# Moving the relative bias products, the first sparse attention jobs and two scalings in a one-core three-block kernel

## The chip, the cores and the metric

The kernel runs on one core of one Trainium2 chip. The metric is the device time of one launch in microseconds (us); lower is better. The core's engines are TensorE (PE in the rows; its weight loads are PEld), VectorE (DVE), ScalarE (ACT), GpSimd (POOL) and SyncE (SP), which here only issues DMAs. Each has its own queue of instructions and waits for the others through semaphores.

## The reference, cut to what matters

The input is 512 tokens of 1024 channels in float32. Three residual mixers follow each other, each with a gated feed-forward behind it:

```python
x = x + conformer_conv(rmsnorm(x))       # pointwise, GLU, 31-tap conv, layer norm, swish, pointwise
x = x + swiglu(rmsnorm(x))
x = x + dilated_attention(rmsnorm(x), rel_bias)   # 12 heads, relative bias from a table of 32 buckets
x = x + swiglu(rmsnorm(x)); x = rmsnorm(x)        # the final norm of the first block
# second block
rq, rk, rv, rg, aq, ak, av, iq, ik, iw = split(rms_norm(h) @ w_in)
ret_out = retention(rq, rk, rv, rg)      # per head: rms over 64 channels, then times silu(rg)
att_out = dsa_attention(aq, ak, av, iq, ik, iw)   # an indexer keeps the top 128 keys per query
h = h + rms_norm(concat(ret_out, att_out) @ w_out)
h = h + rms_norm(swiglu(conv3(rms_norm(h) @ w_up)) @ w_down)
```

## The kernel before, in words

Activations lie transposed: 128 channels on the partitions, 512 tokens on the free axis, eight tiles of X. Every float32 product of the big layers is made of three reduced-precision ones (hi by hi, lo by hi, hi by lo; lines 620 to 622), so that every weight is split: ScalarE copies it to `W_hi` (line 1154), VectorE subtracts to get `W_lo` (line 1821). A layer is a list of units of 256 columns; a unit has two halves of 128 columns, and each half runs over its 8 tiles of the contraction. The weights of a unit are loaded, split and used two units apart.

**Slots.** The last mixer's input layer "inp" has 13 units. PE's order there is written by hand: after each tile k of half h of unit j, a function `beside(g)` is called with the slot number g = 16j + 8h + k, and it issues what else belongs to that slot. ScalarE and VectorE call functions of the same name with the same g, in the same order, and put the evictions of a half (`raw_copy`, `taken`) behind its eighth slot. Nothing ties the engines to a common time but semaphores: each engine works through its own list in order.

**Sparse attention jobs.** There are 16 jobs n (four blocks of 128 queries times four pairs of heads, keys 128, 256, 384 and 512 wide). Job n begins at slot s(n) = 84 + 7n. Its scores are at s+1 on PE, the masked maximum at s+2 on VectorE, the exponentials at s+3 on ScalarE, the reciprocal at s+4 on VectorE and the scaling at s+4 on ScalarE. Its transposes lie at the next job's s and s+2, with ScalarE copies at s+1 and s+3, and its values at the next job's s+4 (PE) with a copy out (ScalarE).

**Beside them** stand, with slots of their own: 48 rounds of the top-k search on VectorE (`choose`, lines 2264 and 2266, slots 66 to 157; 256 keys wide for the first 16 rounds, then 384, then 512), and the retention: scores on PE (line 1045), decay on VectorE (`ret_decay`, line 2301), values on PE (line 1056); after the fourth of each head pair ScalarE takes the sum out (`ret_take`, line 1557, slots 147, 162, 189, 200), PE sums over the heads (`head_sum`, line 1064, slots 148, 163, 190, 201), ScalarE makes the root, and VectorE the reciprocal (`ret_normed`, line 2307, slots 150, 165, 192, 203). The vector queue makes `W_lo` for the unit after next in the slots with g % 16 == 2, ahead of all else in the slot; ScalarE makes `W_hi` at the end of each unit, behind the eviction copy.

```python
                if g % SLOTS == 2 and g > 2 * SLOTS:      # vector, beside(g)
                    split_lo(L, At(g // SLOTS - 1))
                ...
                if r == 2 and 0 <= q < 16:
                    dsa_max(q)
                ...
                if r == 3 and 0 <= q < 16:                # scalar, beside(g)
                    dsa_exp(q)
                ...
                if g - 1 in RET_LAST_AT:
                    ret_take(RET_LAST_AT.index(g - 1))
```

**The bias products** (line 708, three products of a 33 x 4 table with a 33 x 384 one-hot matrix, six matmul records) are issued on PE behind the last tap of the 31-tap convolution and ahead of the layer norm's sums (lines 761, 763, 770). ScalarE copies them out (line 1298), sends them to DRAM (line 1313), loads the Sqrt table and squares the centred tiles. PE waits for the three copies before the first sum of squares. The result is first read for the second mixer.

**The end of "wout"**, the last mixer's output layer: VectorE copies each half to Y (line 2389), multiplies X by the final norm's gain and factor two tiles per unit (line 2412), the last two of them between the two halves of the last `W_lo` (line 2421) and the norm's reciprocal (line 2432), and then adds the normed result to X (lines 2443 and 2446).

Of the kernel before, what the change touches and what calls it, by code (L numbers as in the profile page):

```python
# [7 lines left out]
ACT = mybir.ActivationFunctionType  # L8
# [48 lines left out]
DIAG = 384  # L57
# [56 lines left out]
STAT_AT = SLOTS + 5  # L114
KV_AT = 2 * SLOTS + 4
INDEX_AT = [52, 54, 58, 60, 62, 64, 66, 68, 70, 72, 74, 76]
DSA_AT, DSA_STRIDE = 84, 7
ROUND_AT = [66 + 39 * r // 20 for r in range(48)]
RV_AT = [129, 130, 177, 178]
RET_AT = [134, 137, 140, 143, 149, 152, 155, 158, 180, 182, 184, 186, 191, 193, 195, 197]  # L120
# [56 lines left out]
def build(nc, a, out):  # L177
# [13 lines left out]
    with ctx:  # L191
# [417 lines left out]
        def _(pe):  # L609
# [91 lines left out]
            def bias_products():  # L701

                pe.wait_ge(tab_in, 32)
                pe.wait_ge(pads_set, 2)
                pe.wait_ge(const2_in, 16)
                pe.wait_ge(acc_free, layers["pw2"].base)
                for g in range(3):
                    nc.tensor.matmul(PS[1 + g][0:GROUP_HEADS, 0:DIAG], table[:, GROUP_HEADS * g:GROUP_HEADS * (g + 1)],
                                     onehot[:, g, :], start=True, stop=True).then_inc(fvec_ps, 1)

            def conv_tap(n):
# [44 lines left out]
                            conv_tap(g - FIRST_TAP)  # L756
            for n in range(SLOTS * L.n - FIRST_TAP, len(PE_TAPS)):
                conv_tap(n)
            bias_products()
            pe.wait_ge(ln_sum, 7)  # L760
            nc.tensor.matmul(PS[0][:], ones, SSUM[:], start=True, stop=False)
            pe.wait_ge(conv_made, 6)
            nc.tensor.matmul(PS[0][:], ones, CV[:, 7, :], start=False, stop=True).then_inc(ln_sum_ready, 1)
            pe.wait_ge(fvec_made, 3)
            for n, m in enumerate(LN_SUMS):
                if m == LN_PAIR:
                    pe.wait_ge(xc_made, DT + 1)
                else:
                    pe.wait_ge(xc_sq, m + 1)
                nc.tensor.matmul(PS[1][:], ones, LN_SQ[m % 4], start=(n == 0), stop=(n == len(LN_SUMS) - 1)).then_inc(ln_var_ready, 1)  # L770
            linear("pw2", HID_hi, HID_lo, ready=after(ln_lo_made, 0))

            def three_units(L):
# [292 lines left out]
            def beside(g):  # L1066

                if g == STAT_AT:
                    pe.wait_ge(ssum2, 8)
                    nc.tensor.matmul(AUX[1][:], ones, SSUM2[:], start=True, stop=True).then_inc(stat2_ready, 1)  # L1070
                    rms_sum(FINAL)
                if g == KV_AT:
                    kv_transposes()
                if g in INDEX_AT:
                    index_scores(INDEX_AT.index(g))
                if g in RV_AT:
                    rv_transposes(RV_AT.index(g))
                if g in HEADSUM_AT:
                    head_sum(HEADSUM_AT.index(g))
                if g in RET_LAST_AT:  # L1080
                    ret_values(4 * RET_LAST_AT.index(g) + 3)
                if g in RET_AT:
                    n = RET_AT.index(g)
                    if n % 4:
                        ret_values(n - 1)
                    ret_scores(n)
                q, r = divmod(g - DSA_AT, DSA_STRIDE)
                if r == 0 and 1 <= q <= 16:
                    dsa_transposes(q - 1, 0)
                if r == 1 and 0 <= q < 16:  # L1090
                    dsa_scores(q)
                if r == 2 and 1 <= q <= 16:
                    dsa_transposes(q - 1, 1)
                if r == 4 and 1 <= q <= 16:
                    dsa_values(q - 1)
# [62 lines left out]
        def _(act):  # L1158
# [136 lines left out]
            def take_bias(g):  # L1295

                act.wait_ge(fvec_ps, g + 1)
                nc.scalar.activation(fvec[:, g, :], PS[1 + g][0:GROUP_HEADS, 0:DIAG], ACT.Copy).then_inc(fvec_made, 1)

            for g in range(SLOTS, SLOTS * L.n):  # L1300
                beside_pw1(g)
# [5 lines left out]
                if g >= SLOTS * L.n:  # L1307
                    diagonals(c)
            split_hi(act, L, At(L.n - 1))
            for g in range(3):  # L1310
                take_bias(g)
            act.wait_ge(fvec_made, 3)
            act.dma_start(bias_rows.rearrange("(g h) d -> h g d", h=GROUP_HEADS), fvec[:]).then_inc(rows_out, 16)

            warm_table(ACT.Sqrt)
            for m in range(DT):
                act.wait_ge(xc_made, m + 1)
# [3 lines left out]
            act.wait_ge(ln_var_ready, len(LN_SUMS))  # L1321
            nc.scalar.activation(STD[:], PS[1][:], ACT.Sqrt, bias=epst[:], scale=1.0 / D_MODEL).then_inc(ln_std, 1)
            warm_table(ACT.Silu)
            for m in range(DT):
                act.wait_ge(ln_scaled, m + 1)
                nc.scalar.activation(CV[:, m, :], CV[:, m, :], ACT.Silu, bias=vec("ln_b", m), scale=vec("ln_g", m)).then_inc(ln_act, 1)
                act.wait_ge(ln_act, m + 1)
                nc.scalar.activation(HID_hi[:, m, :], CV[:, m, :], ACT.Copy).then_inc(ln_hi_made, 1)
# [244 lines left out]
            def beside(g):  # L1573

                if g == STAT_AT:
                    act.wait_ge(stat2_ready, 1)
                    nc.scalar.activation(STD[:], AUX[1][:], ACT.Sqrt, bias=eps2t[:], scale=1.0 / D_MODEL).then_inc(std2_made, 1)
                    act.wait_ge(stat_ready, FINAL + 1)
                    nc.scalar.activation(RF[:], AUX[0][:], ACT.Sqrt, bias=epst[:], scale=1.0 / D_MODEL).then_inc(std_made, 1)
                if g - 1 in INDEX_AT:  # L1580
                    index_relu(INDEX_AT.index(g - 1))
                if g - 1 in RV_AT:
                    rv_copy(RV_AT.index(g - 1))
                q, r = divmod(g - DSA_AT, DSA_STRIDE)
                if r == 1 and 1 <= q <= 16:
                    dsa_keys_first(q - 1, 0)
                if r == 3 and 1 <= q <= 16:
                    dsa_keys_first(q - 1, 1)
                if r == 3 and 0 <= q < 16:
                    dsa_exp(q)  # L1590
                if r == 4 and 1 <= q <= 16:
                    dsa_out(q - 1)
                if r == 4 and 0 <= q < 16:
                    dsa_scaled(q)
                if g - 1 in RET_LAST_AT:
                    ret_take(RET_LAST_AT.index(g - 1))
                if g - 1 in HEADSUM_AT:
                    ret_std(HEADSUM_AT.index(g - 1))
                if g == GATE_AT:
                    gate(11, 0)  # L1600
                    gate(11, 1)
                    gate(12, 0)
# [189 lines left out]
        def _(dve):  # L1792
# [525 lines left out]
            def beside(g):  # L2318

                if g % SLOTS == 2 and g > 2 * SLOTS:  # L2320
                    split_lo(L, At(g // SLOTS - 1))
                if g == KV_AT + 1:
                    kv_tokens()
                if g == 3 * SLOTS + 12:
                    nc.vector.tensor_scalar(LEFT0[:], later, -NEG, None, ALU.mult).then_inc(mask_made, 1)
                q, r = divmod(g - DSA_AT, DSA_STRIDE)
                if r == 2 and 0 <= q < 16:
                    dsa_max(q)
                if r == 4 and 0 <= q < 16:
                    dsa_reciprocal(q)  # L2330
                if g in RET_AT:
                    ret_decay(RET_AT.index(g))
                if g - 2 in HEADSUM_AT:
                    ret_normed(HEADSUM_AT.index(g - 2))
                if g in ROUND_AT:
                    choose(ROUND_AT.index(g))
# [38 lines left out]
            def y_steps(name, y0, add):  # L2375
# [2 lines left out]

                def step(j):
                    u = j.plus(L.base)  # L2380
                    for half in range(2):
                        dve.wait_ge(acc_ready, u.v(2, half + 1))
                        m = At(2 * j.c + half, None if j.i is None else j.i * 2)
                        y = Y[:, bass.ds(m.v(), 1), :].rearrange("p o n -> p (o n)")
                        ps = PS[2 * u.parity + half][:]
                        if add:
                            i = nc.vector.tensor_tensor(y, ps, y, ALU.add)
                        else:
                            i = nc.vector.tensor_copy(y, ps)
                        i.then_inc(x_half, 1) if y0 is None else i.then_inc(y_ready, 1)  # L2390
                    if y0 is None:
                        dve.wait_ge(x_half, j.v(2, 16 + 2))
                    else:
                        dve.wait_ge(y_ready, j.v(2, y0 + 2))
                    nc.vector.sem_inc(acc_free, 1)
                    if name != "wout" or j.c < L.n - 1:
                        split_lo(L, j)
                    if name == "wout" and j.c < L.n - 1:
                        final_normed(j.c)
# [26 lines left out]
            def add_normed(n, gain, k, tiles, split):  # L2426

                if split:
                    final_scaled(DT - 2)
                    last_lo(0)  # L2430
                dve.wait_ge(std_made, n + 1)
                nc.vector.reciprocal(R4[:], STD4[:]).then_inc(r_made, 1)
                if split:
                    final_scaled(DT - 1)
                    last_lo(1)
                dve.wait_ge(r_ps, TOKEN_NORMS.index(n) + 1)
                if k == 0:
# [173 lines left out]
```

## Time and profile before

| | |
|---|---|
| median of 3 runs | 1819.21 us (1819.13 to 1819.86) |
| the profiled execution | 1819.52 us |
| its span, first to last instruction | 1817.7 us |
| mean granted TensorE clock | 0.989 |
| PE busy | 1765.9 us of the span |
| DVE, ACT, POOL busy | 1029.6, 707.8, 172.1 us |
| DMA | 164.63 MB, mean 91 GB/s |

The profile is of one execution. A timeline row gives start, duration, engine, line, operation, tiles and, in brackets, how long the engine had stood idle before and what released it. The granted clock is a share of 2.4 GHz. Some 52 us of the span lie outside PE's busy time, the launch and the end among them.

### The profile page before, as it was taken

Reading aid. Unit: us, or ns where it says so; the run is one execution under the profiler, and the core shown is the slowest. Engines: PE = TensorE matmul, PEld = TensorE weight load, DVE = VectorE, ACT = ScalarE, POOL = GpSimd, SP = SyncE. Lnnn points to the kernel's source line nnn. Section 1 sums busy time; section 2 is a strip of 40 time slices with the busy share of each in tenths; the row PEclk is TensorE's granted clock in tenths of the full one; section 3 lists DMA queues with packets and bytes.
Section 4 is the critical chain, followed back from the end, with each engine's and each line's share of the span. In section 5 each row is a group of like instructions: output and inputs, shape, how many; then the busy total and the mean of one; then the engine's idle time right before and its main releaser. Section 6 shows DMA issues by size and latency. Waiting matters only on the chain.

```text
span 1817.7 us, 21121 instructions
## 1 busy us (share of the span) xinstructions
PE 1765.9 (97%) x8106; PEld 1404.2 (77%) x8106; DVE 1029.6 (57%) x1287; ACT 707.8 (39%) x1095; POOL 172.1 (9%) x128
## 2 busy tenths in 40 slices
PE   7999799999999999999999999989999899999997
PEld 6887588888888878778888888756557778888886
DVE  6998664433444555654424444559856677537753
ACT  5655532212233344332212323465564444324431
POOL 0010010000000100110000004471200200000001
PEclk9999999999999999999999999999999999999998
DMA  5210322322232311132312231523112122322221
GB/s 181 70 47 28 99 94 101 115 95 83 102 118 78 124 70 53 65 105 103 127 70 93 92 127 70 153 73 116 50 62 70 70 93 101 119 70 92 101 96 47
DMA packets 28052, 164.63 MB, mean 91 GB/s; under 512 B 4511, under 2 KB 5675, under 8 KB 11596
## 3 DMA queue, kind: packets, MB, share of 16 engines
q1 hardware_dynamic: 25088, 158.11, 24.7%
q10 hardware_dynamic: 2892, 5.55, 1.0%
q8 instruction: 47, 0.77, 0.2%
q14 instruction: 25, 0.20, 0.0%
HBM read 156.28 MB, written 4.47 MB: 88 GB/s over the span
## 4 chain that ended last, share of the span: by engine, by line
PE 88%; DVE 8%; ACT 2%; issue 1%; POOL 1%; DMA 0%; DVEq 0%; SPq 0%; ACTq 0%; POOLq 0%
PE PS L620 26%; PE PS L622 26%; PE PS L621 26%; PE PS L726 1%; PE PS L727 1%; PE PS L725 1%; DVE W_lo L1821 1%; DVE WK L2266 1%; DVE SSUM L2307 1%; DVE TOP L2264 1%; PE PS L1045 1%; ACT W_hi L1154 1%; POOL ISC L1765 1%; PE PS L1056 1%; DVE PS L2443 0%
## 5 line engine op out<-in xcount | busy, mean ns | idle before, releaser
L620 PE MATMUL PS<-H_hi,W_hi 128*128 128x512 f32 x1600 | 641.6, 401 | 18.3 <-DVE H_lo L1801 14.0
L622 PE MATMUL PS<-H_hi,W_lo 128*128 128x512 f32 x1600 | 626.1, 391 | 0.0
L621 PE MATMUL PS<-H_lo,W_hi 128*128 128x512 f32 x1600 | 625.6, 391 | 0.0
L1154 ACT ACTIVATE W_hi<-W_raw 128x2048 fp32r<-128x2048 f32 (+2 forms) x130 | 262.6, 2020 | 674.2 <-PE PS L622 674.2
L620 PEld LDWEIGHTS PS<-H_hi,W_hi 128*128 128x128 f32 x1600 | 301.9, 189 | 105.1 <-issue 41.2
L1821 DVE TENSOR_TENSOR W_lo<-W_raw,W_hi 128x2048 fp32r<-128x2048 f32 (+2 forms) x130 | 331.2, 2548 | 59.5 <-ACT W_hi L1154 59.1
L622 PEld LDWEIGHTS PS<-H_hi,W_lo 128*128 128x128 f32 x1600 | 301.5, 188 | 64.6
L621 PEld LDWEIGHTS PS<-H_lo,W_hi 128*128 128x128 f32 x1600 | 302.2, 189 | 59.5 <-issue 1.2
L620 PE MATMUL PS<-HID_hi,W_hi 128*128 128x512 f32 x640 | 250.3, 391 | 7.5 <-DVE HID_lo L1962 7.4
L622 PE MATMUL PS<-HID_hi,W_lo 128*128 128x512 f32 x640 | 249.7, 390 | 0.0
L621 PE MATMUL PS<-HID_lo,W_hi 128*128 128x512 f32 x640 | 249.7, 390 | 0.0
L1695 POOL TENSOR_TENSOR SSUM<-SSUM,SQ 128x512 f32<-128x512 f32 x43 | 65.5, 1522 | 1345.9 <-ACT SQ L1196 1344.1
L620 PEld LDWEIGHTS PS<-HID_hi,W_hi 128*128 128x128 f32 x640 | 120.7, 189 | 34.0 <-issue 8.5
L621 PEld LDWEIGHTS PS<-HID_lo,W_hi 128*128 128x128 f32 x640 | 120.6, 188 | 25.0
L622 PEld LDWEIGHTS PS<-HID_hi,W_lo 128*128 128x128 f32 x640 | 120.6, 188 | 25.1
L2004 DVE TENSOR_TENSOR T_u<-PS,R 128x512 f32<-128x512 f32 x44 | 30.4, 690 | 155.7 <-PE PS L622 155.7
L2012 DVE TENSOR_TENSOR T_hid<-T_u,T_act 128x512 f32<-128x512 f32 x66 | 45.7, 693 | 81.1 <-ACT T_act L1378 78.5
L1977 DVE TENSOR_TENSOR X<-X,PS 128x512 f32<-128x512 f32 x40 | 27.0, 684 | 113.9 <-PE PS L622 113.7
L1386 ACT ACTIVATE HID_hi<-T_hid 128x512 f32 (+1 forms) x66 | 42.0, 636 | 57.7 <-DVE T_hid L2012 57.7
L1267 ACT ACTIVATE D_hi<-cmat,tap_hi 128x128 fp32r<-128x128 f32 x108 | 42.1, 390 | 32.2 <-PE PS L727 31.5
L1801 DVE SCALAR_TENSOR_TENSOR H_lo<-X,vecs,H_hi 128x512 fp32r<-128x512 f32 x40 | 36.2, 914 | 27.4 <-ACT H_hi L1181 27.2
L1870 DVE SCALAR_TENSOR_TENSOR CV<-U,vecs,CV 128x512 f32<-128x512 f32 x66 | 50.1, 759 | 0.1
(289 smaller groups left out, 1522.0 us busy)
## 6 DMA issues: line engine op xcount, KB each, us to landing
W_raw<-in_inp SPq DMA_DIRECT2D x13, 1024.0 KB, 4.8
W_raw<-in_pw SPq DMA_DIRECT2D x11, 1024.0 KB, 4.8
W_raw<-in_gu0a SPq DMA_DIRECT2D x11, 1024.0 KB, 4.8
W_raw<-in_gu0b SPq DMA_DIRECT2D x11, 1024.0 KB, 4.8
W_raw<-in_gu1a SPq DMA_DIRECT2D x11, 1024.0 KB, 4.8
W_raw<-in_gu1b SPq DMA_DIRECT2D x11, 1024.0 KB, 4.8
W_raw<-in_gu2a SPq DMA_DIRECT2D x11, 1024.0 KB, 4.8
W_raw<-in_gu2b SPq DMA_DIRECT2D x11, 1024.0 KB, 4.8
```

The lines of the kernel that those rows point to most:

```text
L620: nc.tensor.matmul(dst[:], wh, x_hi[:, k, :], start=(k == first), stop=False)
L621: nc.tensor.matmul(dst[:], wh, x_lo[:, k, :], start=False, stop=False)
L622: return nc.tensor.matmul(dst[:], wl, x_hi[:, k, :], start=False, stop=(k == last))
L1154: nc.scalar.activation(W_hi[b][:, 0:n], W_raw[b][:, 0:n], ACT.Copy).then_inc(w_hi, 1)
L1267: last = nc.scalar.activation(dst[c % 3][:, x, :], ident, ACT.Copy, scale=w)
L1386: nc.scalar.activation(dst, T_hid[:], ACT.Copy).then_inc(hid_hi_made, 1)
L1695: nc.gpsimd.tensor_tensor(SSUM[:], SSUM[:], SQ[:, m.parity, :], ALU.add).then_inc(ss_made, 1)
L1801: nc.vector.scalar_tensor_tensor(out=dst, in0=src, scalar=scale, in1=hi, op0=ALU.mult, op1=ALU.subtract).then_inc(h_lo_made, 1)
L1821: nc.vector.tensor_tensor(W_lo[b][:, 0:n], W_raw[b][:, 0:n], W_hi[b][:, 0:n].bitcast(F32), ALU.subtract).then_inc(w_lo, 1)
L1870: i = nc.vector.scalar_tensor_tensor(out=dst, in0=src, scalar=w, in1=dst, op0=ALU.mult, op1=ALU.add)
L2004: nc.vector.tensor_tensor(T_u[:], PS[2 * b + 1][:], R[:], ALU.mult).then_inc(acc_free, 1)
L2012: nc.vector.tensor_tensor(T_hid[:], T_u[:], T_act[:], ALU.mult).then_inc(hid_made, 1)
```

## The change

Three things change. The bias products are issued behind the layer norm's sums of squares and go to PSUM banks 2 to 4 (they went to 1 to 3), ScalarE's copies and the DMA stand behind the layer norm's root and the loading of the Silu table, and PE waits for the copies ahead of the layer "pw2". The first four sparse attention jobs begin at slots 94, 99, 104 and 109, the others at 116 + 7(n - 4), four slots later than before. The last two scalings of X are issued ahead of the wait for the last unit of "wout".

```diff
-DSA_AT, DSA_STRIDE = 84, 7
+DSA_STARTS = [94, 99, 104, 109] + [116 + 7 * n for n in range(13)]
+DSA_SLOT = {s + r: (n, r) for n, s in enumerate(DSA_STARTS) for r in range(5)}
...
-                    nc.tensor.matmul(PS[1 + g][0:GROUP_HEADS, 0:DIAG], table[:, GROUP_HEADS * g:GROUP_HEADS * (g + 1)],
+                    nc.tensor.matmul(PS[2 + g][0:GROUP_HEADS, 0:DIAG], table[:, GROUP_HEADS * g:GROUP_HEADS * (g + 1)],
...
-            bias_products()
             pe.wait_ge(ln_sum, 7)
...
-            pe.wait_ge(fvec_made, 3)
             for n, m in enumerate(LN_SUMS):
...
+            bias_products()
+            pe.wait_ge(fvec_made, 3)
             linear("pw2", HID_hi, HID_lo, ready=after(ln_lo_made, 0))
...
-                q, r = divmod(g - DSA_AT, DSA_STRIDE)
+                q, r = DSA_SLOT.get(g, (-1, -1))
...
             split_hi(act, L, At(L.n - 1))
-            for g in range(3):
-                take_bias(g)
-            act.wait_ge(fvec_made, 3)
-            act.dma_start(bias_rows.rearrange("(g h) d -> h g d", h=GROUP_HEADS), fvec[:]).then_inc(rows_out, 16)
...
             warm_table(ACT.Silu)
+            for g in range(3):
+                take_bias(g)
+            act.wait_ge(fvec_made, 3)
+            act.dma_start(bias_rows.rearrange("(g h) d -> h g d", h=GROUP_HEADS), fvec[:]).then_inc(rows_out, 16)
...
                 def step(j):
                     u = j.plus(L.base)
+                    if name == "wout" and j.c == L.n - 1:
+                        final_normed(j.c)
...
                 if split:
-                    final_scaled(DT - 2)
                     last_lo(0)
...
                 if split:
-                    final_scaled(DT - 1)
                     last_lo(1)
```

The lookup `DSA_SLOT.get` replaces the `divmod` on PE, ScalarE and VectorE alike.

## Rows read from the trace of the kernel before

**Rows 1.** The page, its fourth part: the chain that ended last, by engine

```profile
PE 88%; DVE 8%; ACT 2%; issue 1%; POOL 1%; DMA 0%; DVEq 0%; SPq 0%; ACTq 0%; POOLq 0%
```

**Rows 2.** Waits of PE from 1150 to 1425 us: total, times, longest

```profile
PE PS L1012 <- ACT E L1530: 7.9, 4, 5.2
PE PS L1056 <- DVE A L2301: 2.3, 2, 1.5
...
PE PS L1064 <- ACT RQK L1558: 0.5, 1, 0.5
```

**Rows 3.** Stretches: length, busy and count per engine, granted clock, DMA share, GB/s

```profile
1220.00:1225.00 5.00, 5.00 (x15) 3.44 (x16) 2.50 (x11) 1.20 (x7) 3.05 (x3) 0.50 0.22 54
1301.00:1304.00 3.00, 3.00 (x10) 1.35 (x12) 1.50 (x4) 0.00 (x0) 0.96 (x1) 0.50 0.25 60
1385.00:1392.00 7.00, 7.00 (x33) 5.79 (x32) 5.79 (x8) 3.22 (x4) 0.00 (x0) 1.00 0.00 0
```

**Rows 4.** Timeline around the layer norm's sums, all engines

```profile
169.90 1.30 POOL L1717 TENSOR_TENSOR SSUM<-SSUM,CV 128x512 f32<-128x512 f32 x1 [2.02 <-DVE CV L1889]
...
177.56 2.10 PE L708 MATMUL PS<-onehot,table 33*4 33x384 f32 x6
177.74 0.69 DVE L1889 TENSOR_TENSOR CV<-CV,PS 128x512 f32<-128x512 f32 x1 [1.29 <-PE PS L727]
...
179.05 0.48 ACT L1298 ACTIVATE fvec<-PS 4x384 f32<-4x384 f32 x1 [0.17 <-PE PS L708]
...
180.55 1.02 PE L763 MATMUL PS<-CV,cmat 128*128 128x512 f32 x2
...
181.69 4.87 DVE L1943 SCALAR_TENSOR_TENSOR CV<-PS,CV 128x512 f32<-128x512 f32 x8 [3.26 <-PE PS L763]
...
194.93 0.81 ACT L1326 ACTIVATE CV<-CV,vecs 128x512 f32<-128x512 f32 x1 [2.63 <-DVE CV L1954]
```

**Rows 5.** Timeline at the end of the layer "wout", VectorE and PE

```profile
1425.32 0.69 DVE L2389 COPY Y<-PS 128x512 f32<-128x512 f32 x1 [3.46 <-PE PS L622]
...
1428.49 0.72 DVE L2412 SCALAR_TENSOR_TENSOR X<-X,vecs,RF 128x512 f32<-128x512 f32 x1
1428.62 1.16 PE L685 MATMUL PS<-cmat,R 128*128 128x128 f32 x8 [0.57 <-DVE R L2432]
1429.12 1.22 DVE L2421 TENSOR_TENSOR W_lo<-W_raw,W_hi 128x1024 fp32r<-128x1024 f32 x1
1430.26 0.75 DVE L2443 SCALAR_TENSOR_TENSOR PS<-Y,vecs,PS 128x512 f32<-128x512 f32 x1
```

**Rows 6.** From the eviction of slot 79's half to slot 98: one stretch, then timeline

```profile
1210.80:1232.60 21.80, 16.60 (x70) 11.65 (x69) 16.74 (x46) 9.80 (x22) 13.12 (x10) 0.84 0.29 85
...
1218.60 0.69 DVE L2207 TENSOR_TENSOR RQK<-PS,CS 128x512 f32<-128x512 f32 x1 [0.63 <-ACT T_act L1492]
1219.21 0.15 DVE L2289 RECIPROCAL RDEN<-DEN 128x2 f32<-128x2 f32 x1
1219.85 0.48 PE L1012 MATMUL PS<-cmat,E 128*128 128x128 f32 x1 [5.20 <-ACT E L1530]
...
1230.37 2.28 DVE L1821 TENSOR_TENSOR W_lo<-W_raw,W_hi 128x2048 fp32r<-128x2048 f32 x1
...
1242.58 1.90 ACT L1154 ACTIVATE W_hi<-W_raw 128x2048 fp32r<-128x2048 f32 x1
```

**Rows 7.** Timeline around the first head sum, slots 142 to 149

```profile
1279.36 0.57 ACT L1522 ACTIVATE E<-PS,NEGMAX 128x384 f32<-128x384 f32 x1
...
1280.26 0.49 PE L1045 MATMUL PS<-RQK 64*128 64x128 f32 x4
...
1284.24 0.60 ACT L1557 ACTIVATE SSUM<-PS 128x512 f32<-128x512 f32 x1 [0.19 <-PE PS L1056]
...
1285.07 3.37 DVE L1821 TENSOR_TENSOR W_lo<-W_raw,W_hi 128x2048 fp32r<-128x2048 f32 x1
...
1285.96 0.59 PE L1064 MATMUL PS<-SSUM,cmat 128*128 128x512 f32 x1
...
1289.74 0.56 DVE L2283 CUSTOM_DVE_ANT_0 PS<-PS,LEFT 128x384 f32<-128x384 f32 x1
```

More of the change, by code:

```diff
@@ L1297, in take_bias @@
                 act.wait_ge(fvec_ps, g + 1)
-                nc.scalar.activation(fvec[:, g, :], PS[1 + g][0:GROUP_HEADS, 0:DIAG], ACT.Copy).then_inc(fvec_made, 1)
+                nc.scalar.activation(fvec[:, g, :], PS[2 + g][0:GROUP_HEADS, 0:DIAG], ACT.Copy).then_inc(fvec_made, 1)
             for g in range(SLOTS, SLOTS * L.n):
@@ L1583, in beside @@
                     rv_copy(RV_AT.index(g - 1))
-                q, r = divmod(g - DSA_AT, DSA_STRIDE)
+                q, r = DSA_SLOT.get(g, (-1, -1))
                 if r == 1 and 1 <= q <= 16:
@@ L2325, in beside @@
                     nc.vector.tensor_scalar(LEFT0[:], later, -NEG, None, ALU.mult).then_inc(mask_made, 1)
-                q, r = divmod(g - DSA_AT, DSA_STRIDE)
+                q, r = DSA_SLOT.get(g, (-1, -1))
                 if r == 2 and 0 <= q < 16:
```

## The prediction

> **What bounds the kernel now.** I read the chain that ended last first: it lies on PE for 88% and on VectorE for 8% [rows 1], so a part of the change counts only where PE stops or where VectorE stands in the chain. Then PE's waits in the last mixer: 7.9 us in four waits for the scaled exponentials, 5.2 of them at once, 2.3 for retention's decay and 0.5 at a head sum [rows 2]. Then stretches for what a wait costs behind it: after the wait of 5.2 the granted clock is 0.50, half of 2.4 GHz, over the 5 us from 1220, and 0.50 again after the waits near 1300 [rows 3]; 5 us at half cost 2.5 us of work. Where PE only multiplies at the full clock, 33 matmuls touch 7.00 us [rows 3], so a slot of three takes about 0.69 us. Last the timelines of the places that the edits touch, to see which queue is late there.
>
> **Bias products.** Now six matmuls run from 177.56 for 2.1 us, while VectorE's last tile of the convolution is complete at 177.74 + 0.69 = 178.43; the matmul that needs it starts only at 180.55, and 1.14 us later VectorE centres the tiles [rows 4]. The other operand of the sums is older: GpSimd's last addition ended at 171.2 [rows 4]. Without the bias products that matmul starts near 178.6, so 1.9 us go (at most 2.1, the products themselves; at least 1.6, if a weight load follows the wait). Everything up to the first Silu moves along. Put back, the products lie in PE's idle time behind the sums of squares, and cost PE nothing. ScalarE's three copies (0.48 each with 0.17 before it, 2.0 together) and a DMA issue of about 0.3 fall into the 2.63 us in which it waits before the first Silu at 194.93 [rows 4]. If that cover were gone, the overhang would be paid in full; 0.3 us at most. Term: **-1.9**.
>
> **Scalings of X.** In the wait of 3.46 us before the copy at 1425.32 there is room for both. Now the second scaling starts at 1428.49, the half of W_lo behind it at 1429.12, and the first multiplication of the norm at 1430.26 [rows 5]. Taken out, it frees 0.63 us, but the multiplication also reads the spread factor, which PE finishes at 1428.62 + 1.16 = 1429.78 [rows 5]: late next. So 0.4 us go (0.3 to 0.6). The first scaling was hidden by ScalarE's copy and stays worth nothing. Term: **-0.4**.
>
> **Sparse attention jobs.** No work is added. What changes is which part of another queue PE must wait for, so I take the places in order.
>
> *The transposes of job 0.* They were at slot 91 and needed VectorE up to slot 88; now they are at slot 99 and need the reciprocal at slot 98, behind that slot's W_lo. From the eviction at 1210.8 to the end of that W_lo at 1232.6 VectorE was busy for 16.74 of 21.8 us [rows 6]. I take 4.3 of the 5.1 us as waits for pieces of jobs 0 and 1 and the rest as gaps between short instructions, and 0.7 of the work is no longer in front. So it gets there at 1227.6 at the earliest, and PE 0.64 later (from reciprocal to transposes, 1219.21 to 1219.85 [rows 6]): 1228.3. PE stood at the transposes from 1219.85 - 5.20 = 1214.65. Without the early scores (0.5) but with 0.3 more wait for an eviction it is through slot 91 at 1214.4, and with four slots and the scores at 1217.6. There it needs the eviction of slot 87, which began at 1218.60 behind 0.6 of waiting and the 0.4 of a maximum [rows 6], and will end at 1218.4: 0.8 of wait. Four slots on, at 1221.2, it stands at the transposes: a wait of **7.1** where 5.2 was, with the same half clock behind it. At the stride of 5 only one slot is left between scaling and transposes, which costs job 2 another 0.3; and its second copy now stands behind the raw copy (0.6) and W_hi (1.90 [rows 6]) of the unit that ends at slot 111 and takes 0.3 itself, where PE needs 1.5 for two slots and a transpose: 1.3. Together 7.1 + 0.8 + 0.3 + 1.3 = 9.5 (6 to 11).
>
> *The first head sum, slot 148.* This is the heart of the forecast. ScalarE takes retention's sum out at slot 147. Before, no job stood directly in front. Now job 8 begins at 144: its exponentials are at 147, ahead of the take, and wait for its maximum at slot 146, which stands behind that slot's W_lo. From the start of retention's scores at 1280.26 to W_lo at 1285.07 are 4.8 us, 4.7 without a reciprocal. Then follow W_lo 3.4, the maximum 1.1 (two of 0.56), the exponentials 1.1 (two of 0.57) and the take 1.1 (two of 0.60, overlapped) with 0.2 for hand-overs [rows 7]: 11.6 in all. PE got to its head sum 5.7 us after the scores (1285.96 - 1280.26 [rows 7]); with the other pieces that now lie between, 6.0. A wait of 5.6. W_lo took 3.37 here and 2.28 at 1230.37 [rows 6, 7]; with 2.28 the wait is 4.5. I take **5.0**, between the two.
>
> The Trainium skill, "SBUF — State Buffer", section "SBUF: two separate sides", says that a VectorE operation with two SBUF inputs and a GpSimd one lock each other out of a shared pair of ports for a whole instruction. By that rule the long W_lo is one that met GpSimd's rotation of the same unit, and the sum is 0.6 higher if they meet again and 0.5 lower if not.
>
> Behind this wait comes a half clock as after the 5.2: 2.5. VectorE stands still meanwhile, since the next decay needs scores that PE issues after the head sum; that may add a us at the values of slot 155, which I leave to the range.
>
> *Both places together.* New: waits 9.5 + 5.0, half clock 2.5 + 2.5, 19.5 in all. Old: the waits for exponentials 7.9 and the longest for a decay 1.5 [rows 2], half clock 2.5 behind the first and some 1.3 for the 3 us at 1301 [rows 3], 13.2 in all. Term: **+6.3** (1 to 11).
>
> *The later head sums.* At slot 162 the take stands behind job 9's scaling, and this behind a reciprocal that follows W_lo. If the queues are level there as in rows 7, W_lo 2.3, reciprocal 0.2, scaling 1.2, take 1.1 and hand-overs 0.2 make 5.0 against PE's 3.7 for three slots and two products: **+1.3** (0 to 2.5). At slot 189 it stands behind job 13's second copy and job 14's exponentials, which are wider than those of rows 7: some 3.3 us against PE's 1.7, +1.6. In return the second decay wait (0.8 of the 2.3) and the wait at the last head sum (0.5) go [rows 2], because no values and copy-out stand before the last take: **+0.3** (-1.3 to 2; three Silus now stand behind the last job's copy-out ahead of the next layer's input, and can cost up to 1).
>
> **Sum.** -1.9 - 0.4 + 6.3 + 1.3 + 0.3 = +5.6, so 1819.5 + 5.6 = **1825.1 us**, against the profiled execution's 1819.52. That one lies 0.3 above the median, 1819.21, which is nothing beside these terms.
>
> **Rivals.** (a) *Faster.* The wait of 5.2 and its half clock go and nothing takes their place: VectorE works through the rounds without stopping for jobs 0 and 1 and gets through slot 98 some 5 us sooner [rows 6]. Its place is slots 91 to 99, its price 5.2 + 2.5 = 7.7, with the other parts 10.0: 1809.5. It decides if VectorE keeps that lead through the jobs at stride 5, so that the maximum of job 8 is done before PE reaches slot 147. Against it: the retention's scores at slot 143 tie VectorE to PE again, and W_lo and the maximum come after them. Chance 0.17. (b) *No change.* The vector queue with its 48 rounds sets the pace and waits only move: the job part gives 0, give or take 3, the total 1819.5 - 2.3 = 1817.2. For it: the old waits for a decay are waits for VectorE [rows 2]. Against it: its lead from slot 98 is lost again while it waits for PE. Chance 0.20. (c) *The forecast*, slower by one or both of the first two waits: 0.63. That the jobs don't move is excluded: all three engines read the same table.
>
> **How the numbers follow.** The forecast's own range is 1820 to 1831, from the bounds of its terms, not all at their ends at once. The range of all is 1812 to 1831: it leaves out most of (a), about 0.12, and 0.07 above. A difference of 0.2% (3.6 us) is about what a measurement of this kernel can tell from none. Faster 0.17, same 0.20, slower 0.63.
>
> **What would show it.** Bias: the six matmuls near 189, centring at 179.8, the first Silu still waiting. Scalings: the norm's multiplication 0.4 sooner after the copy. Jobs: a PE wait of about 7 at line 1012 in place of 5.2; a wait of 4 to 6 at line 1064 for the take, with clock 0.50 behind it. If line 1064 waits for less than 1 us the central step is wrong, and (a) or (b) holds.

## The result and the profile after

The changed kernel takes **1832.13 us** (median of 4 runs, 1831.18 to 1832.63) against 1819.17 us: the ratio is 1.007, with a 95% interval of 1.0054 to 1.0086. That is 13.0 us slower, where 5.6 were forecast and the range ended at 1831. The profiled execution took 1832.5 us, with a span of 1830.7. Some line numbers differ by one or two from those of before: L621 to L623 are the matmuls of the linear layers, L1013 the transposes of the sparse attention, L1065 the head sum, L1057 retention's values.

The page, its first and fourth part, after:

```profile
PE 1769.7 (97%) x8106; PEld 1408.3 (77%) x8106; DVE 1030.4 (56%) x1287; ACT 707.8 (39%) x1095; POOL 174.3 (10%) x128
...
PE 89%; DVE 7%; ACT 2%; issue 1%; POOL 1%; DMA 0%; SPq 0%; DVEq 0%; ACTq 0%; POOLq 0%
```

The instructions are the same in number, and the shares of the chain are nearly those of [rows 1]: this is a matter of when PE stands still, and at which clock it then runs. The waits of PE from 1150 to 1425 us, after (total, times, longest), to be held against [rows 2]:

```profile
PE PS L1013 <- ACT E L1530: 8.8, 1, 8.8
PE PS L1065 <- ACT RQK L1558: 8.0, 3, 4.8
PE PS L1057 <- DVE A L2301: 3.0, 3, 2.0
PE PS L621 <- DVE H_lo L2358: 2.4, 1, 2.4
PE PS L1022 <- ACT PT L1538: 1.2, 1, 1.2
PE PS L621 <- DVE RQK L2207: 0.7, 1, 0.7
PE PS L621 <- DVE AQ L2205: 0.3, 1, 0.3
```

They sum to 24.4 us; before it was 12.2 (the 10.7 of [rows 2] and 1.5 at the first matmul of "wout"). So the waits of PE in the last mixer grew by 12 us, nearly as much as the kernel got slower. The stretches behind three of them, and one at the spread of the last norm's factor (columns as in [rows 3]: length, busy and count per engine, granted clock, DMA share, GB/s):

```profile
1228.00:1236.00 8.00, 7.46 (x24) 4.90 (x25) 4.01 (x15) 2.21 (x10) 1.10 (x1) 0.55 0.37 131
...
1292.00:1298.00 6.00, 5.48 (x18) 2.41 (x18) 0.00 (x0) 2.69 (x5) 0.00 (x0) 0.62 0.20 83
...
1392.00:1399.00 7.00, 6.76 (x23) 5.51 (x24) 6.80 (x12) 4.07 (x8) 0.00 (x0) 0.76 0.01 2
1441.00:1446.00 5.00, 2.08 (x8) 1.78 (x8) 3.87 (x6) 1.13 (x2) 0.00 (x0) 0.50 0.46 162
```

The third is the first work of "wout": 23 matmuls in 7 us behind a wait of 2.4 us, where 33 ran in [rows 3]. In the fourth, eight small matmuls take 2.08 us that took 1.16 in [rows 5].

**The bias part.** Timeline around the layer norm's sums, after:

```profile
177.30 0.69 DVE L1889 TENSOR_TENSOR CV<-CV,PS 128x512 f32<-128x512 f32 x1 [1.29 <-PE PS L728]
...
178.04 1.13 PE L763 MATMUL PS<-CV,cmat 128*128 128x512 f32 x2
179.28 4.88 DVE L1943 SCALAR_TENSOR_TENSOR CV<-PS,CV 128x512 f32<-128x512 f32 x8 [1.29 <-PE PS L763]
...
187.59 2.09 PE L709 MATMUL PS<-onehot,table 33*4 33x384 f32 x6
...
189.80 1.20 ACT L1299 ACTIVATE fvec<-PS 4x384 f32<-4x384 f32 x3
...
192.52 0.81 ACT L1326 ACTIVATE CV<-CV,vecs 128x512 f32<-128x512 f32 x1 [1.52 <-DVE CV L1954]
```

From VectorE's last tile to the centring it is now 179.28 - 177.30 = 1.98 us, where it was 181.69 - 177.74 = 3.95 [rows 4]: 1.97 gained. The three copies take 1.20 and lie in ScalarE's idle time; 1.52 us of it are left before the first Silu.

**The scalings.** Timeline at the end of "wout", after:

```profile
1432.15 2.73 DVE L2414 SCALAR_TENSOR_TENSOR X<-X,vecs,RF 128x512 f32<-128x512 f32 x4
...
1441.24 2.08 PE L686 MATMUL PS<-cmat,R 128*128 128x128 f32 x8 [0.56 <-DVE R L2433]
1443.35 0.76 DVE L2443 SCALAR_TENSOR_TENSOR PS<-Y,vecs,PS 128x512 f32<-128x512 f32 x1 [1.06 <-PE PS L686]
```

VectorE now has time to spare (1.06 us idle), but the spread that it waits for ran at half clock, so nothing was gained.

**The first place.** Timeline of job 0 on all engines, after:

```profile
1222.43 0.30 DVE L2283 CUSTOM_DVE_ANT_0 PS<-PS,LEFT 128x128 f32<-128x128 f32 x1 [0.64 <-DVE RQK L2207]
...
1222.71 1.26 POOL L1745 TENSOR_TENSOR RQK<-RQK,TS 128x512 f32<-128x512 f32 x1
1222.89 1.23 DVE L2249 SCALAR_TENSOR_TENSOR ISC<-cmat,ISC 128x128 f32<-128x128 f32 x1
...
1225.29 2.68 DVE L1821 TENSOR_TENSOR W_lo<-W_raw,W_hi 128x2048 fp32r<-128x2048 f32 x1
1225.97 3.13 POOL L1745 TENSOR_TENSOR RQK<-RQK,TS 128x512 f32<-128x512 f32 x1
1227.89 0.15 DVE L2289 RECIPROCAL RDEN<-DEN 128x2 f32<-128x2 f32 x1
...
1228.54 0.47 PE L1013 MATMUL PS<-cmat,E 128*128 128x128 f32 x1 [8.79 <-ACT E L1530]
```

The reciprocal stands right behind W_lo, as forecast, and 0.65 us behind it PE gets its transposes, having waited 8.79 us.

**The first head sum.** Timeline of slots 146 to 148, after:

```profile
1286.32 2.77 DVE L1821 TENSOR_TENSOR W_lo<-W_raw,W_hi 128x2048 fp32r<-128x2048 f32 x1
...
1289.49 0.59 DVE L2283 CUSTOM_DVE_ANT_0 PS<-PS,LEFT 128x384 f32<-128x384 f32 x1
...
1290.17 0.58 ACT L1522 ACTIVATE E<-PS,NEGMAX 128x384 f32<-128x384 f32 x1 [3.38 <-DVE NEGMAX L2283]
...
1291.77 0.60 ACT L1558 ACTIVATE RQK<-PS 128x512 f32<-128x512 f32 x1
...
1292.52 1.19 PE L1065 MATMUL PS<-SSUM,cmat 128*128 128x512 f32 x1 [4.76 <-ACT RQK L1558]
```

This is the chain that the prediction wrote down: W_lo, maximum, exponentials, take, head sum.

### The profile page after: what moved, and what is told of

Same layout as the page of the kernel before. It is cut to its first block, busy times and chain, and to the rows that moved or that the text cites. A ratio compares the mean times of both kernels' runs of the same rounds, so it can differ in the third digit from the quotient of the medians.

```text
span 1830.7 us, 21121 instructions
## 1 busy us (share of the span) xinstructions
PE 1769.7 (97%) x8106; PEld 1408.3 (77%) x8106; DVE 1030.4 (56%) x1287; ACT 707.8 (39%) x1095; POOL 174.3 (10%) x128
## 4 chain that ended last, share of the span: by engine, by line
PE 89%; DVE 7%; ACT 2%; issue 1%; POOL 1%; DMA 0%; SPq 0%; DVEq 0%; ACTq 0%; POOLq 0%
PE PS L621 27%; PE PS L623 26%; PE PS L622 26%; PE PS L728 1%; PE PS L726 1%; PE PS L727 1%; DVE W_lo L1821 1%; PE PS L1022 1%; ACT W_hi L1155 1%; PE PS L1046 1%; POOL ISC L1765 1%; DVE PS L2443 0%; DVE X L2446 0%; PE PS L1001 0%; PE PS L852 0%
## 5 line engine op out<-in xcount | busy, mean ns | idle before, releaser
L621 PE MATMUL PS<-H_hi,W_hi 128*128 128x512 f32 x1600 | 643.7, 402 | 19.4 <-DVE H_lo L1801 13.3
L623 PE MATMUL PS<-H_hi,W_lo 128*128 128x512 f32 x1600 | 626.9, 392 | 0.0
L621 PEld LDWEIGHTS PS<-H_hi,W_hi 128*128 128x128 f32 x1600 | 302.5, 189 | 107.2 <-issue 44.0
L623 PEld LDWEIGHTS PS<-H_hi,W_lo 128*128 128x128 f32 x1600 | 302.3, 189 | 64.8
L621 PE MATMUL PS<-HID_hi,W_hi 128*128 128x512 f32 x640 | 251.0, 392 | 5.5 <-DVE HID_lo L1962 5.4
L623 PE MATMUL PS<-HID_hi,W_lo 128*128 128x512 f32 x640 | 250.2, 391 | 0.0
L621 PEld LDWEIGHTS PS<-HID_hi,W_hi 128*128 128x128 f32 x640 | 120.8, 189 | 31.8 <-issue 6.4
L623 PEld LDWEIGHTS PS<-HID_hi,W_lo 128*128 128x128 f32 x640 | 120.8, 189 | 25.2
```

The lines of the kernel that those rows point to most:

```text
L621: nc.tensor.matmul(dst[:], wh, x_hi[:, k, :], start=(k == first), stop=False)
L623: return nc.tensor.matmul(dst[:], wl, x_hi[:, k, :], start=False, stop=(k == last))
```

## The experiments

Each run was timed beside the kernel before on the same chip, and the ratio goes against that kernel's times there (medians 1819.95 us for e1 to e4, 1819.84 for e5 to e8, 1819.45 for e9 to e12).

| run | median us | ratio | 95% interval |
|---|---|---|---|
| e1_jobs_alone | 1832.34 | 1.0067 | 1.0053 to 1.0081 |
| e2_bias_alone | 1818.53 | 0.9992 | 0.9983 to 1.0001 |
| e3_scalings_alone | 1819.65 | 0.9999 | 0.9990 to 1.0008 |
| e4_no_jobs | 1818.30 | 0.9990 | 0.9981 to 0.9999 |
| e5_late_rest | 1827.87 | 1.0045 | 1.0028 to 1.0061 |
| e6_late_four | 1816.24 | 0.9981 | 0.9971 to 0.9990 |
| e7_take_first | 1822.00 | 1.0012 | 1.0002 to 1.0021 |
| e8_both_first | 1818.82 | 0.9993 | 0.9983 to 1.0002 |
| e9_four_take | 1815.86 | 0.9979 | 0.9970 to 0.9988 |
| e10_end_back | 1828.98 | 1.0050 | 1.0035 to 1.0065 |
| e11_rounds | 1810.60 | 0.9952 | 0.9938 to 0.9965 |
| e12_rounds_before | 1820.60 | 1.0006 | 0.9997 to 1.0015 |

### Which part costs

Theory 1: the new places of the jobs cost more than the whole change, and the two other parts give a little back. Rivals: the parts depend on each other, or the clock takes their gain. First the kernel before with the jobs' places alone:

```diff
-DSA_AT, DSA_STRIDE = 84, 7
+DSA_STARTS = [94, 99, 104, 109] + [116 + 7 * n for n in range(13)]
+DSA_SLOT = {s + r: (n, r) for n, s in enumerate(DSA_STARTS) for r in range(5)}
```

> The kernel before with the new places of the jobs alone. Theory 1 (the jobs cost what the change cost, and more): the traces put the last mixer at +12.5 us (from -1.66 at its first slots to +10.85 at the first matmul of wout), so the time is about 1819.2 + 12.5 + 1.3 of half clock at wout's start = 1833 (range 1831 to 1835), with the wait of 8.8 us at the transposes of job 0, 4.8 at the first head sum and 2.0 at the decay. Rival (the place of the four first jobs matters only together with the earlier arrival that the bias part gave): the waits are shorter and the time is below 1829. Rival of the prediction on record (the jobs cost 7.9): 1827.

Then the bias part's lines of the change alone, the scalings' lines alone, and both (the change with `DSA_STARTS = [84 + 7 * n for n in range(17)]`):

> The kernel before with the relative bias products behind the sums of the layer norm alone. Theory 1: the gain is what the two traces show behind pw2's start, 1.2 to 1.6 us (the centring comes 1.9 earlier, a longer half-clock stretch in pw2 gives 0.8 back, the three copies ahead of the first Silu take 1.5 but are waited for either way): 1817.6 to 1818.0. Rival (all of 1.9 to 2.4 stays): 1817.0. Rival (the cold stretch in pw2 takes the whole gain): 1819.2.

> The kernel before with the two scalings of X ahead of the wait alone. Theory 1: 0.4 earlier at the reciprocal, nothing else: 1818.8. Rival (the half clock at the spread of the reciprocal, 2.08 against 1.16 us in the change, comes with the earlier reciprocal): 1819.5 to 1820.0. Rival (no effect; the half clock came from the jobs' shift): 1819.2.

> The change without the jobs' new places: bias part and scalings together. Theory 1: the sum of the two alone, 1817.2 to 1817.6 (-1.6 and -0.4), and the new places are then worth the rest, +14.5 to +15. Rival (the parts interact, so that the jobs have another price with them than without): this run and the one with the jobs alone don't add up to the +12.96 of the change, by more than 1 us.

The jobs alone cost 12.2 us (9.6 to 14.7), with the same waits in the trace as the change: 9.1 at the transposes, 8.0 at head sums, 3.0 for the decay, 2.4 at "wout". The bias part gains 1.5, its interval touching zero; of the scalings nothing can be seen; both together gain 1.8 (0.2 to 3.5). With the jobs that adds to 10.4 against the change's 12.7 (by its ratio), within the intervals. So the cost is the jobs', and whether the parts add to better than 2 us these runs can't say: by the medians, e1 and e4 together fall 2.2 us short of the change, more than the 1 us that e4's rival names, but the five runs of e1 alone spread over 5.2 us.

The times expected for e2, e3 and e4 were missed by 0.5 to 0.9 us; set against the 1819.95 of before beside them, the differences are as expected (-1.4, -0.3 and -1.7). Both of e3's rivals on the half clock at the spread fall by the traces: the eight small matmuls took 1.16 us in e3, where the scalings alone are moved, and 2.08 in e1, e2 and e4. Neither the earlier scalings nor the jobs' places are needed for it.

### Which of the jobs' places costs

The change with its first four jobs back, the later ones still four slots late:

```diff
-DSA_STARTS = [94, 99, 104, 109] + [116 + 7 * n for n in range(13)]
+DSA_STARTS = [84, 91, 98, 105] + [116 + 7 * n for n in range(13)]
```

> The changed kernel with its first four jobs back at slots 84, 91, 98 and 105; the later ones stay four slots behind their old places. Theory 1 (most of the cost comes from the later jobs' order among the scores, where the take for the head sum stands behind a job's exponentials): the first places wait as before (6.5 us in all at 84 to 112), the later ones as in the change (14.0 us with wout's start, before 7.0), and the half clock behind the first head sum and at wout's start stays: 1817.5 + 7.0 + 1.7 + 1.3 = 1827.5. Rival (the crowding of the first four is what costs, since VectorE's queue is then behind until the end): the head sum's wait of 4.8 us is gone and the time is below 1822.

And the other way round: the later ones at their old slots, the first four late and five slots apart:

```diff
-DSA_STARTS = [94, 99, 104, 109] + [116 + 7 * n for n in range(13)]
+DSA_STARTS = [92, 97, 102, 107] + [112 + 7 * n for n in range(13)]
```

> The changed kernel with the jobs from the fifth on at their old slots 112 + 7n and the first four at 92, 97, 102 and 107 (five slots apart, as in the change, two earlier, so that the maximum and the reciprocal of job 0 stand ahead of the low copy of the weights at slot 98). Theory 1: the head sums and the decay wait as before (5.0 us less than in the change and 3 of half clock and of wout's start), and the first place costs at most what it does in the change, 3.4 of waits and 1.7 of half clock over before: 1820 to 1823. Rival (the crowding shifts everything behind): the head sum at slot 148 waits 3 us or more and the time is above 1826.

e5 came out at 1827.9 where 1827.5 was expected: with the first four at home, the head sum still waited 4.8 us and the decay 2.0. Four slots later for the jobs from the fifth on cost some 10 us by themselves (1827.9 against e4's 1818.3). e6 did better than either theory: 1816.2 us, faster than before. The longest waits of PE from 1150 to 1425 us in e6:

```profile
PE PS L1013 <- ACT E L1530: 7.0, 3, 5.1
PE PS L1057 <- DVE A L2301: 2.3, 2, 1.5
PE PS L621 <- DVE H_lo L2358: 1.5, 1, 1.5
PE PS L1065 <- ACT RQK L1558: 0.8, 2, 0.5
...
```

So crowding the first four costs nothing that can be seen. Two slots earlier than in the change job 0's reciprocal is ahead of W_lo (slot 98), and its wait is 5.1 us instead of 8.8.

### Which instruction in front

The change with ScalarE's take moved ahead of the job pieces of its slot:

```diff
+                if g - 1 in RET_LAST_AT:
+                    ret_take(RET_LAST_AT.index(g - 1))
                 q, r = DSA_SLOT.get(g, (-1, -1))
...
-                if g - 1 in RET_LAST_AT:
-                    ret_take(RET_LAST_AT.index(g - 1))
```

> The changed kernel with ScalarE's take for the head sum issued ahead of that slot's job pieces, all slots as they are. Theory 1 (the order on ScalarE is what the head sums wait for): the waits of the three head sums fall from 8.0 us to under 2, the half clock at the first of them to what it was before: 1832 - 6 - 1.7 = 1824 (range 1822 to 1826). Rival (VectorE's queue is the cause; the take waits for tiles that VectorE makes late, whatever stands before it): the waits stay above 5 us, time above 1829.

And in addition W_lo behind the maximum and the reciprocal of its slot:

```diff
-                if g % SLOTS == 2 and g > 2 * SLOTS:
-                    split_lo(L, At(g // SLOTS - 1))
...
                 if r == 4 and 0 <= q < 16:
                     dsa_reciprocal(q)
+                if g % SLOTS == 2 and g > 2 * SLOTS:
+                    split_lo(L, At(g // SLOTS - 1))
```

> As the run with the take first, and VectorE's low copy of the weights (slot 98, 106 and so on) issued behind the slot's maximum and reciprocal of a job instead of ahead of them. Theory 1 (job 0's transposes wait behind the low copy, 2.7 us long there): its wait of 8.8 us falls by 2 to 3 us, and the half clock there with it, so 2 to 4 us below the run with the take first. Rival (the low copy is then late for the next matmuls, or job 0 is late for another reason): the wait moves to the matmuls that need the low copy, and the time is the same as with the take first within 1 us.

One call moved up gives 10 us back (1832.1 to 1822.0). ScalarE's timeline in e7:

```profile
1285.37 0.60 ACT L1557 ACTIVATE SSUM<-PS 128x512 f32<-128x512 f32 x1 [2.22 <-PE PS L1057]
...
1289.50 0.58 ACT L1522 ACTIVATE E<-PS,NEGMAX 128x384 f32<-128x384 f32 x1 [2.77 <-DVE NEGMAX L2283]
```

The take no longer waits for the maximum, and no wait of PE at L1065 is left. A new one of 1.1 us for the normalisation's root (L1565, behind a job's copy and scaling on ScalarE) takes a part back, and the waits for a decay are nearly what they were, 2.7 us for 3.0. In e8 the reciprocal goes first:

```profile
1225.37 0.15 DVE L2289 RECIPROCAL RDEN<-DEN 128x2 f32<-128x2 f32 x1
1225.44 2.69 DVE L1821 TENSOR_TENSOR W_lo<-W_raw,W_hi 128x2048 fp32r<-128x2048 f32 x1
...
1226.02 0.48 PE L1013 MATMUL PS<-cmat,E 128*128 128x128 f32 x1 [6.24 <-ACT E L1530]
```

The wait is 6.24 where it was 8.74 in e7, and the kernel 3.2 us faster; the matmuls that need W_lo don't wait for it. Both orders of instructions are shown as causes, of the waits at the head sums and of a part (2.5 us) of the wait at job 0's transposes.

### The end

```diff
-DSA_STARTS = [94, 99, 104, 109] + [116 + 7 * n for n in range(13)]
+DSA_STARTS = [94, 99, 104, 109] + [116 + 7 * n for n in range(7)] + [163 + 5 * n for n in range(2)] + [175, 182, 189, 196]
```

> The changed kernel with its last jobs back at their old slots (the jobs from the twelfth on start at 163, 168, 175, 182 and 189, instead of 165, 172, 179, 186 and 193). Theory 1 (the cost is local, and the one at the end comes from the last job ending four slots later): the waits from slot 180 on fall from 5.1 us (1.7 + 0.3 + 0.7 + 2.4) to the 2.9 of before (0.8 + 0.5 + 1.5), and wout starts at full clock (1.3): 1832.1 - 2.2 - 1.3 = 1828.6. Rival (the wait at wout's start comes from what was late earlier): it stays at 2.4, and the time is above 1831.

PE's timeline in e10, and below it the stretch behind its last line:

```profile
1330.83 0.44 PE L1013 MATMUL PS<-cmat,E 128*128 128x128 f32 x2 [1.57 <-ACT E L1530]
...
1391.92 0.47 PE L621 MATMUL PS<-H_hi,W_hi 128*128 128x512 f32 x1 [1.54 <-DVE H_lo L2358]
```

```profile
1391.90:1398.90 7.00, 6.98 (x31) 5.72 (x32) 6.75 (x12) 4.08 (x8) 0.00 (x0) 1.00 0.01 2
```

The wait at "wout" is back to 1.54 and the layer starts at full clock (though it did so in e5 too, behind 2.43 us: 30 matmuls in 7 us at a clock of 1.00). The two squeezed jobs cost 1.57 us of wait of their own, which was not expected, and still it is some 3 us faster than the change: the end's cost is local.

### A version that beats both

e9 puts e6's places and e7's order together. e11 adds earlier places for VectorE's first sixteen selection rounds; e12 gives those to the kernel before, alone:

```diff
-ROUND_AT = [66 + 39 * r // 20 for r in range(48)]
+ROUND_AT = list(range(66, 82)) + [66 + 39 * r // 20 for r in range(16, 48)]
```

> The run with the first four jobs at 92, 97, 102 and 107 (1816.2 us), with ScalarE's take for the head sum issued first as well. Theory 1 (the waits add place by place): the head sums' remaining waits, 0.5 and 0.3 us, go: 1815.4. Rival (the take ahead delays a job's exponentials and so VectorE's and TensorE's later work by as much): 1816.2 or above.

> The run of the same call with the first four jobs at 92 to 107 and the take first, and VectorE's sixteen selection rounds of the first block at slots 66 to 81, one in each, instead of up to slot 95: they then run in the 7.3 and 1.9 us in which VectorE waits for ScalarE's copies. Theory 1 (job 0's maximum waits behind those rounds: the queue was busy without a gap for 9 us ahead of it): it comes some 3 us earlier, the reciprocal about 3, the wait of 5.1 us at its transposes falls to about 2.3, and with a shorter wait some of the half clock goes too: 1815.5 - 2.8 = 1812.7 (range 1811 to 1813.5). Rival (the job then waits as long for ScalarE's copies or its exponentials): within 0.5 of the run without.

> The kernel before with the sixteen rounds at slots 66 to 81 alone. Theory 1: there job 0's reciprocal (slot 88) stands behind VectorE's take of the half unit that ScalarE copies late (slot 87), so the wait of 5.2 us stays within 0.3, and the time is 1819.2 to 1819.9, no change: earlier rounds pay only with the later places. Rival (the rounds in the queue were what it waited for): the wait falls by 2 us or more, 1817.5 or less.

e9 is 1815.9 us, between the two expectations, which can't be told apart at that size. e11 is **1810.6 us**, 8.8 us (6.4 to 11.3) faster than before. VectorE and PE in e11:

```profile
1208.44 0.69 DVE L2205 SCALAR_TENSOR_TENSOR AQ<-PS,CS 128x512 f32<-128x512 f32 x1 [3.33 <-ACT T_u L1492]
...
1211.25 0.73 DVE L2269 TENSOR_TENSOR LEFT<-ISC,WK 128x256 f32<-128x256 f32 x1
1212.01 1.26 DVE L2272 TENSOR_SCALAR LEFT<-LEFT 128x256 f32<-128x256 f32 x1
...
1216.00 0.28 DVE L2283 CUSTOM_DVE_ANT_0 PS<-PS,LEFT 128x128 f32<-128x128 f32 x1
...
1220.06 0.33 PE L1013 MATMUL PS<-cmat,E 128*128 128x128 f32 x1 [2.21 <-ACT E L1530]
```

The rounds fill the time in which VectorE waits for a copy of ScalarE (3.33 us left of 7.26). Job 0's maximum comes at 1216.0, in e9 at 1219.94, of which 1.3 us are from earlier on; the wait is 2.2, in e9 5.0. The same work, 112 matmuls from one take of half a unit to job 3's transposes, in e9 and in e11:

```profile
1217.35:1248.60 31.25, 25.44 (x112) 16.40 (x113) 26.49 (x78) 15.20 (x47) 14.66 (x11) 0.89 0.34 108
```

```profile
1216.22:1242.47 26.25, 23.25 (x112) 14.93 (x112) 21.83 (x64) 15.37 (x47) 13.77 (x11) 1.00 0.50 155
```

PE is idle 5.8 us in the one and 3.0 in the other, and busy 25.4 and 23.3: behind the shorter wait the clock stays at 2.4 GHz, and that gives 2.2 us more. The expectation had the wait right and put next to nothing for the clock, so the time came out below its range.

e12 shows no gain, as its first theory has it, but its wait is longer than before, 6.36 against 5.20, where it was expected within 0.3, and the time of 1820.6 lies above the 1819.9 expected at most:

```profile
1218.65 0.28 DVE L2283 CUSTOM_DVE_ANT_0 PS<-PS,LEFT 128x128 f32<-128x128 f32 x1
...
1220.68 0.69 DVE L2207 TENSOR_TENSOR RQK<-PS,CS 128x512 f32<-128x512 f32 x1 [1.43 <-ACT T_act L1492]
1221.29 0.16 DVE L2289 RECIPROCAL RDEN<-DEN 128x2 f32<-128x2 f32 x1
1221.93 0.48 PE L1012 MATMUL PS<-cmat,E 128*128 128x128 f32 x1 [6.36 <-ACT E L1530]
```

At its old place job 0's maximum (slot 86) stands behind W_lo as before, and now also behind the two steps of LEFT that follow the sixteenth round (0.72 and 1.24 us in e12). Of the two sets of places tried, earlier rounds pay only with the jobs' later ones.

## Why the prediction was wrong in size

The time lies above the stated range. The direction was right, and so were the mechanisms of the two largest waits; wrong was what was taken off for the old waits. The terms are taken in their order.

- **Bias, -1.9:** right. 1.97 at the centring; 1.5 alone on the clock. In the profile of after the next layer starts 2.4 us earlier (0.4 of them were there ahead of this place), but then runs at half clock for 5.7 us instead of 4.0, which eats some 0.8.
- **Scalings, -0.4:** the instructions moved as said, but the spread took 2.08 us instead of 1.16, so this place lost 0.8 us in the profile of after. That is not the scalings' doing (1.16 in e3, 2.08 in e1 and e2); what sets it stays open. Alone the term is not measurable.
- **First place:** the first wait was put at 7.1 and is 8.8. The profile of after is 1.7 us ahead there, so that its reciprocal, at 1227.89, is 2.0 late against "So it gets there at 1227.6 at the earliest"; that missed a gap of 0.64 us ahead of the maximum, a mask of 1.23 us (0.29 was its length before) and a W_lo of 2.68 (2.28 in [rows 6]). The smaller waits came to 2.1, against 2.4 forecast. Together 10.9 for 9.5.
- **First head sum, 5.0:** 4.76, the best of the steps, down to the chain.
- **Old waits counted as gone:** this is the step that failed. "Old: the waits for exponentials 7.9 and the longest for a decay 1.5" took the decay's 1.5 off, and no reason is given for it; one of 2.03 us stands at the same place, slot 155. The prediction left "a us at the values of slot 155" to the range, because VectorE stands still behind the head sum. It does (busy 0.00 from 1292 to 1298), but that is not the cause: in e7 the head sum doesn't wait and VectorE is idle for only 0.57 us, yet 1.76 of the 2.03 stay. PE in after, then VectorE and PE in e7:

```profile
1307.80 0.87 PE L1057 MATMUL PS<-A,RVT 128*64 128x384 f32 x4 [2.03 <-DVE A L2301]
```

```profile
1294.12 3.35 DVE L2307 RECIPROCAL SSUM<-STD 128x512 f32<-128x512 f32 x1 [0.57 <-ACT STD L1565]
...
1301.17 0.87 PE L1057 MATMUL PS<-A,RVT 128*64 128x384 f32 x4 [1.76 <-DVE A L2301]
```

From the decay of slot 149 to the end of that of slot 152 VectorE needs 10.1 us before, 9.6 in after and 10.2 in e7, with at most 0.6 idle, and a reciprocal of 3.3 us lies in it each time. The change didn't move that work. Before, PE met it in two waits, 1.38 for job 9's scaled exponentials (a part of the 7.9; their scaling stood behind this reciprocal) and then 1.48 for the decay; the first went with the job's new place, and the second grew. That this is one and the same delay is read from the traces; no run takes the reciprocal away. In the same way "the second decay wait (0.8 of the 2.3)" was taken off, and waits of 0.33 and 0.65 came.

- **Later head sums, +1.3 and +1.6:** 1.55 and 1.70.
- **The end:** the three Silus behind the last copy-out, "can cost up to 1", also left to the range, cost 0.9; e10 took it away. The start of "wout" at a clock of 0.76 came on top in after, but not in e5 behind the same wait.
- **Half clock:** the forecast had 1.2 more than before. Set side by side by their copies of W_hi, the change is 1.7 us ahead at 1209 and 12.2 behind at 1395. Waits, added singly, explain 12.0 of these 13.9 us, which leaves 1.9, put down to the clock by difference.

The waits alone are 5.4 us above those in the sum: 1.4 at the first place, 2.0 at the decay, 1.0 at the later decays, 0.9 at "wout", 0.1 at the three head sums together. With 0.7 of clock in the mixer, 1.2 at the scalings and some 0.3 at the bias part that makes 7.6 of the missing 7.4. Two places with a known sign, the decay of slot 155 and the Silus, stood in the range and not in the sum: 2.9 us together, both of the same sign.

Of the rivals, "faster" had its point of decision right: the lead that VectorE would have to keep until slot 147. e7 shows that the order on ScalarE was enough to decide it. "Waits only move" fell as a price of nothing, for PE's waits grew by 12 us; at slot 155 it was right.

**W_lo and GpSimd.** The Trainium skill, "SBUF — State Buffer", section "SBUF: two separate sides", was cited for W_lo: if the two met again the sum would be 0.6 higher. They met: W_lo took 2.77 us, 0.5 over the 2.28 of [rows 6] (the rotation of GpSimd in front ended 0.6 us after its start), so the effect is there and was less than the 1.1 us of [rows 7].

## What to carry to other kernels

When a piece of work is moved in interleaved queues, write down for each engine what stands directly in front of what the busy engine waits for; one call moved up in ScalarE's order gave back 10 us here, of the 12 that the new slots cost. Count old waits place by place: before one is taken off, name the work that it waits for and where that work goes (the reciprocal of 3.3 us stayed, and so did the wait). A wait left "to the range" with a known place belongs in the sum. Fill an engine's idle time ahead of a late operand with work that has nothing to do with it (the rounds of e11), before shifting the work that waits.

## What the runs showed of the hardware

**VectorE and GpSimd hold each other up.** The mask on VectorE (L2249, 128x128) takes 0.29 us alone. After the change it began at 1222.89, while an addition of GpSimd ran from 1222.71 to 1223.97, took 1.23 us and ended at 1224.12. GpSimd's next addition, begun at 1225.97 during W_lo, took 3.13 us where its like take 1.26, and ended 1.1 us behind W_lo's end at 1227.97. In e11 the two steps of LEFT, between additions of GpSimd, took 0.73 and 1.26 us, against 0.42 and 0.29 in after. The rounds (MAX8, one input) ran at their usual 0.43 next to GpSimd. The Trainium skill's section "SBUF: two separate sides" ("SBUF — State Buffer") has the two engines lock each other out for a whole instruction; the trace agrees, in both directions, and here it made a mask four times as long.

**The half clock depends on more than the wait.** A wait of 5.0 us in e9 was followed by 0.50 over 5 us, one of 2.2 in e11 by none. At the start of "wout" the same wait of 2.43 us had a clock of 0.76 over 7 us behind it in after and of 1.00 in e5; one of 1.5 (e10) had 1.00. Behind the same wait in front of "pw2" the clock was 0.52 from 198 to 201 us in after and 0.79 in e6, whose code up to there is the same (and whose layer began 1.2 us later). So the single runs of one kernel can differ by some us (e4: 1815.3 to 1819.8) with nothing different in the kernel; what sets the clock behind one and the same wait was not tried.
